# Other starting bytes for the two halves of the streamed weights in a two-block float32 model

## What is computed

```python
x = first_block(x, ...)     # h = rmsnorm(x); x + mixed @ w_out; x + conv_ffn(rmsnorm(x), up, down)
x = second_block(x, ...)    # twice: u = rmsnorm(x) @ w_in; three attentions; gates; x + y @ w_out
```

## The kernel before

| buffer | begins at | past a multiple of 64 | past a multiple of 128 |
|---|---|---|---|
| raw | 8320 | 0 | 0 |
| w_hi | 41088 | 0 | 0 |
| w_lo | 57472 | 0 | 0 |
| x | 73856 | 0 | 0 |
| h_offset (32 bytes, never used) | 90240 | 0 | 0 |
| h | 90272 | 32 | 32 |
| mixed | 123040 | 32 | 32 |
| shared | 155808 | 32 | 32 |
| ab_hi | 171648 | 0 | 0 |
| ab_lo | 172896 | 32 | 96 |
| sq_hi, sq_lo, sums_r | 219872, 221920, 223968 | 32 | 96 |

## Time and profile before

### The profile page before, as it was taken

How to read it: one execution, slowest core, us unless ns; L and a number is a source line. 1 busy time by engine, 2 the same in 40 slices (tenths; PEclk the granted TensorE clock), 3 DMA queues, 4 the chain that set the end, 5 groups by cost and what they waited for, 6 DMA issues and landing times. The chain is left out here.

```text
span 3365.0 us, 72929 instructions
## 1 busy us (share of the span) xinstructions
PE 3323.8 (99%) x27834; PEld 3283.5 (98%) x27834; DVE 2185.9 (65%) x3568; ACT 1705.3 (51%) x2787; POOL 310.4 (9%) x314
## 2 busy tenths in 40 slices
PE   8999999999999999999999999999999999999999
PEld 7999999999999998899999999999899999999999
DVE  7667666656656666678655665665777755666665
ACT  5555644434434455655544554444665654554443
POOL 1010100000000025011002200001012101210000
PEclk9999999999999999999999999999999999999999
DMA  5234455555555554344455545554444445445554
GB/s 190 107 112 148 176 184 190 188 187 186 189 187 187 187 187 163 136 163 160 158 197 185 183 160 188 188 200 178 145 153 163 156 173 209 175 163 188 187 206 162
DMA packets 90629, 584.28 MB, mean 174 GB/s; under 512 B 10480, under 2 KB 11120, under 8 KB 28400
## 3 DMA queue, kind: packets, MB, share of 16 engines
q1 hardware_dynamic: 88992, 577.47, 48.1%
q0 software_dynamic: 1488, 4.72, 0.4%
HBM read 580.05 MB, written 2.10 MB: 173 GB/s over the span
## 5 line engine op out<-in xcount | busy, mean ns | idle before, releaser
L172 DVE TENSOR_TENSOR w_lo<-raw,w_hi 128x768 fp32r<-128x768 f32 (+5 forms) x1202 | 1379.3, 1160 | 374.0 <-ACT w_hi L161 367.0
L191 PE MATMUL bank<-h,w_hi 128*128 128x256 f32 x5168 | 1461.2, 283 | 15.2 <-DVE w_lo L172 11.8
L161 ACT ACTIVATE w_hi<-raw 128x768 fp32r<-128x768 f32 (+4 forms) x1190 | 1095.8, 968 | 694.5 <-PE bank L193 616.9
L192 PE MATMUL bank<-h,w_hi 128*128 128x256 f32 x5168 | 1444.1, 279 | 0.0
L193 PE MATMUL bank<-h,w_lo 128*128 128x256 f32 x5168 | 1443.8, 279 | 0.0
L191 PEld LDWEIGHTS bank<-h,w_hi 128*128 128x128 f32 x5168 | 973.2, 188 | 21.1 <-DVE w_lo L172 10.2
L192 PEld LDWEIGHTS bank<-h,w_hi 128*128 128x128 f32 x5168 | 973.4, 188 | 2.9 <-issue 1.9
L193 PEld LDWEIGHTS bank<-h,w_lo 128*128 128x128 f32 x5168 | 973.1, 188 | 0.0
L191 PE MATMUL bank<-mixed,w_hi 128*128 128x256 f32 x2272 | 634.5, 279 | 0.7 <-DVE w_lo L172 0.7
L192 PE MATMUL bank<-mixed,w_hi 128*128 128x256 f32 x2272 | 633.9, 279 | 0.0
L193 PE MATMUL bank<-mixed,w_lo 128*128 128x256 f32 x2272 | 633.9, 279 | 0.0
(11 more groups left out here) (404 smaller groups left out, 3323.1 us busy)
## 6 DMA issues: line engine op xcount, KB each, us to landing
raw<-in_w SPq DMA_DIRECT2D x485, 1024.0 KB, 4.8
raw<-in_w_br SPq DMA_DIRECT2D x96, 512.0 KB, 3.9
raw<-in_w_uq SPq DMA_DIRECT2D x8, 768.0 KB, 4.3
raw<-in_w_ukv SPq DMA_DIRECT2D x8, 512.0 KB, 3.2
bias_t<-in_bias POOLq DMA_DIRECT2D x16, 192.0 KB, 4.2
x<-in_x SPq DMA_DIRECT2D x4, 512.0 KB, 7.7
raw<-in_w_kr SPq DMA_DIRECT2D x4, 512.0 KB, 3.5
out_x<-x SPq DMA_DIRECT2D x3, 512.0 KB, 7.7
```

The costliest lines, as they stand in the source:

```text
L161: act.activation(w_hi[:, b % 2, c], raw[:, b, c], ACT.Copy).then_inc(S["hi_done"], 1)
L172: dve.tensor_tensor(w_lo[:, b % 2, c], raw[:, b, c], w_hi[:, b % 2, c].bitcast(F32), ALU.subtract).then_inc(S["lo_done"], 1)
L191: pe.matmul(o, w_hi[:, b % 2, c], a_hi, start=start and k == t0, stop=False)
L192: pe.matmul(o, w_hi[:, b % 2, c], a_lo, start=False, stop=False)
```

## The change

Two spacers are added and one is made smaller. A spacer is a buffer that nothing reads or writes. `w_offset` has 6 floats (24 bytes), `lo_offset` 12 floats (48 bytes), and `h_offset` goes from 8 floats (32 bytes) to 6 (24 bytes). By the sizes alone w_hi is meant to begin 24 bytes past a multiple of 64, w_lo 24 + 48 = 72, so 8 past one, and h and mixed 72 + 24 = 96, so 32 past one. No instruction, loop, wait or transfer is added, removed or moved.

```diff
         raw = sb("raw", [4, UNIT])
+        w_offset = sb("w_offset", 6)
         w_hi = sb("w_hi", [2, UNIT], F32R)
+        lo_offset = sb("lo_offset", 12)
         w_lo = sb("w_lo", [2, UNIT], F32R)
         x = sb("x", [KT, SEQ])
-        h_offset = sb("h_offset", 8)
+        h_offset = sb("h_offset", 6)
         h = sb("h", [KT, 2 * SEQ], F32R)
         mixed = sb("mixed", [KT, 2 * SEQ], F32R)
```

## The result

The changed kernel takes 3440.71 us (median of 4 runs, 3439.09 to 3441.0) against 3368.85 us before: ratio 1.0213, interval 1.020 to 1.0225. It is slower, as forecast, but by 72 us where 36.5 were forecast, and it lies above the range of 3368 to 3412.

The account below looks back on a forecast made before the run. TensorE's matmul pitch was taken to bound the kernel; 39.9 (unit weight loads) - 2.7 (reverse roles) - 0.7 (slack) = +36.5 us gave 3403.2 on the profiled execution, 3405.0 us as median, range 3368 to 3412.

Parts of the forecast that it names:

- The bound: Whole kernel: TensorE's gapless matmul pitch of 116.67 ns sets the time; starting bytes act only through it.
- The pitch of the units: Units' weight-loading matmuls: pitch rises from 116.67 to 118.30 ns, on 24,480 matmuls, +39.9 us.
- The second witness: Lines 1353 to 1355, h streaming from 32, loaded starts varying: mean pitch 117.9 ns, taken to support 118.3.
- The wish for a multiple of 64: Unit matmuls: the loaded operand's start matters and wants a multiple of 64 bytes; 1.63 ns more without it.
- The reverse roles: head_values and latent_values, loading from 0 and streaming from 32: 1632 matmuls fall from 118.30 to 116.67 ns, -2.7 us.
- Slack: Windows 33.4 to 461 and 1261.6 to 1429: PE's waits hide some slowdown, at most 6.7 us, taken -0.7 us.
- Splits and loads: ScalarE and VectorE weight splitting and transfers into raw: no cost from the new starts, taken as nothing.
- a third keeps its pitch: Unit tiles: distance modulo 128 counts, so two of three matmuls pay; +24.8 us, 3393.4 us, chance 0.16.
- No change: Unit matmuls: the operands' distance stays 32, so pitch stays 116.67 ns and time 3368.5 us; chance 0.11.
- The dearer case: Unit weights pay the dearest tile's price of lines 1353 to 1355: +81 us, 3450 us, chance 0.08.
- Faster: Unit matmuls: activations streaming from 0 cross fewer 64-byte pieces, pitch falls toward 115 ns; -39 us, 3329 us, chance 0.06.
- The words: Buffers really start at 24, 8 and 32 as the change says: pitch 117.9 ns, +31 us, 3399 us, chance 0.03.

Follow-up runs that it names:

- e13_same64: Kernel before with both weight halves at 32, h and mixed at 0 past a multiple of 64, distance from weights to activations -32: 3400.87 us.
- e3: Changed kernel's starts, but w_lo at 32 instead of 96 past a multiple of 128 (distance +96 for both weight halves): 3438.39 us.
- e5: Kernel before with h at 64 and mixed at 96 past a multiple of 128, weights still at 0: 3396.93 us.
- e14: Kernel before with h at distance 160 and mixed at 224 from the weights, which stay in place: 3399.22 us.
- e1_h0: Kernel before with only h and mixed moved, from 32 to 0 past a multiple of 64: 3442.96 us.
- e7_shift32: Kernel before with both weight halves moved to 32, h to 64 and mixed to 96 past a multiple of 128: 3371.62 us.
- e4_words: Kernel before with w_hi really at 24 and w_lo at 8 past a multiple of 64, cut from larger buffers, h and mixed at 32: 3427.09 us.
- e12_p192: Kernel before with h and mixed both at distance 192 from the weights, which stay in place: 3341.16 us, ratio 0.9916.

## Why the prediction was right and wrong

- **The bound**: right. Only the pitch moved, in the stretch without gaps and nearly everywhere else. Of the signs of being wrong that the prediction named, a pitch above 119 came, and PE's idle time in front of its unit line stayed at 15.2 us.
- **Where the buffers go**: right. The words 24 and 8 did not come true; the starts are 32, 32 and 0 past a multiple of 64.
- **The pitch of the units**: this term failed. 1.63 ns were taken from head_values, "just this pair, with the tensors' names exchanged"; 3.33 were measured. The pair was the same in remainders of 64 only. Exchanging the roles turns the distance round: 0 - 32 = -32 there, while the changed kernel has 256 - 160 = +96 (h at 90368, w_hi at 41120, remainders of 512). At -32 units do have 118.3 ns (e13_same64), at +96 they have 120.0 (e3, e5, head_values in e14). The second witness was none: lines 1353 to 1355 walk through sixteen distances, and their mean of 117.9 agreed by luck. The 48 steps take 5.66 us before, in the changed kernel and in e13_same64, and 5.67 in e1_h0, whatever the units do. Nor is 33.88 to 34.24 their dearest tile: the one from 38.12 to 38.49 takes 361 ns, 120.3 a step.
- **The wish for a multiple of 64**: wrong. e1_h0 keeps the weights on theirs and pays 120.0; e7_shift32 takes them off and has 117.2.
- **The reverse roles**: -2.7 us were forecast, and 118.4 instead of 116.7 came. Their distances are now -96 for w_hi and -32 for w_lo, with 117.9 and 118.3 in the table, not +32.
- **Slack**: 0.7 us was taken. The span grew by 7.4 us less than 24,480 x 3.33 ns, at twice the extra pitch; 2.6 of these are waits, within the bound of 6.7. The other 4.7 are no slack but a sum that counts too much: some 690 unit matmuls have no back-to-back step behind them, and between the waits ahead of 460.97 such a step grew by 2.9 ns only. In e13_same64, which has the forecast pitch, the shortfall is 24,480 x 1.65 - 1632 x 1.5 - (3398.9 - 3365.0) = 4.0 us, 1.9 of it waits; it is most of what that run stays below 3405.
- **Splits and loads**: right, 1519 and 1262 ns.
- **The rivals**: "a third keeps its pitch" had the right kind of cause, the distance, with 128 for 256, and the wrong consequence: with w_lo at a distance of 32 (changed) and of 96 (e3) the pitch is 120.0 alike. "No change" rested on the distance as well, but took +32 and -32 for equal. The dearer case (3450) was nearest in time and given 0.08: its 120 ns was read from the dearest tile of lines 1353 to 1355 and held too rare. That was luck as well: this tile's distances are 192 and 224, which the units hold at 113.3 to 118.3, and in the changed kernel, with the same distances, it takes 0.35 us (33.34 to 33.69). "Faster" falls with e1_h0, where the activations alone move to a multiple of 64 and the pitch rises to 120.0. "The words" gave 3399 us; e4_words, at these starts, took 3427.09.
- **The range**: it ended at 3412 because the price was known for one distance only. The bounds of the pitch, 115 and 120 ns, held; the range should have reached the upper one (3368.55 + 81 - slack).

The Trainium skill, page "TensorE: Matmul & The Clock Gate", section "Step-by-step: what each phase is for", says of the two read ports of TensorE: "Loading the next tile's weights doesn't steal SBUF read bandwidth from the running matmul." The traces do not bear out that loading leaves the running matmul alone: with the same instructions, sizes and clock, the pitch goes from 113.3 to 120.0 ns by where the two operands begin. Whether it is read bandwidth that is lost, no run here tells.

## What to carry to other kernels

Where TensorE's matmuls with freshly loaded weights set the time, the starts of the two operands are a parameter: 3% of the time between the best and the worst kernel tried here, with not one instruction changed. Set it by the distance from loaded to streamed operand over one period (256 bytes here), measure every step of 32, and check in the built program where buffers really begin. Give both halves of the weights the same distance as long as no run has shown what a mixture costs, and time more than one stretch, since one distance can have two rhythms. A row counts as a model of another case only if the whole address relation is the same, its sign too.

## What was not expected of the hardware

- The pitch of 256-column float32r matmuls, each with its load of 128 columns, depends on the distance of the operands modulo 256 bytes: in the long stretch 120.0 ns at 0 and 96, 116.7 at 32 (but 120.0 in one stretch of e7), 118.3 at 224.
- Some distances have two stable rhythms; at 64 and at 192 they are 113.3 and 117.8 ns, 4% apart, each kept for tens to hundreds of us. The runs of e12_p192 scatter more than those of the changed kernel (4.7 us in five against 1.9 in four); that the rhythms are the reason is not shown.
- A pitch slower by 3.33 ns made the 461 us ahead of the long stretch only 3.9 us longer, not 9.1: 2.8 us came back from waits and other steps, and 2.4 had never been added.

That the two reads, of the next weights and of the running matmul's activations, meet in the same part of SBUF is what a distance rule suggests; no run here shows the place where they meet.
